# A gated recurrence in a three-layer kernel: states between chunks of 128 tokens in place of two levels of scores

## The reference

```python
# S_t = diag(f_t) S_(t-1) + k_t v_t^T,  o_t = S_t^T q_t,  k_t = 1 - f_t
G = jnp.cumsum(log_f, axis=3)            # within a chunk
q_dec, k_inv = q * jnp.exp(G), k * jnp.exp(-G)
k_to_end = k * jnp.exp(G_last - G)
o_intra = tril(q_dec @ k_inv.T) @ v
def step(state, xs):
    o_inter = jnp.einsum('bhtd,bhdv->bhtv', q_c, state)
    new_state = decay_c.T * state + jnp.einsum('bhsd,bhsv->bhdv', k_c, v_c)
    return new_state, o_inter
...
o = o * rsqrt(mean(o * o) + eps) * norm_g * sigmoid(o_gate)
```

## Time and profile before

| | us |
|---|---|
| median of three runs | 1473.52 |
| lowest, highest | 1471.86, 1474.23 |
| span of the profiled execution | 1473.2 |
| TensorE matmuls busy in it | 1439.7 |
| VectorE busy | 959.1 |
| ScalarE busy | 867.1 |
| GpSimd busy | 64.6 |

### The profile page before, as it was taken

How to read it: one execution, slowest core, us unless ns; L and a number is a source line. 1 busy time by engine, 2 the same in 40 slices (tenths; PEclk the granted TensorE clock), 3 DMA queues, 4 the chain that set the end, 5 groups by cost and what they waited for, 6 DMA issues and landing times.

```text
span 1473.2 us, 25050 instructions
## 1 busy us (share of the span) xinstructions
PE 1439.7 (98%) x10188; PEld 933.4 (63%) x10188; DVE 959.1 (65%) x1928; ACT 867.1 (59%) x1250; POOL 64.6 (4%) x150
## 2 busy tenths in 40 slices
PE   7999999999999999999999999989999999899998
PEld 4444477566468448576688764646785755466677
DVE  6732556888589666565677423678667246799974
ACT  6554456777654665454563553557665466778863
POOL 0000000000000100000010000001000000000000
PEclk9999999999999999999999999999999999999999
DMA  6323223113322423342323223321134332100002
GB/s 193 108 92 114 86 94 104 62 58 115 114 87 86 160 87 128 109 137 86 115 86 114 88 87 97 105 86 31 33 98 133 118 115 86 58 2 2 2 5 98
DMA packets 128531, 131.93 MB, mean 90 GB/s; under 512 B 9913, under 2 KB 125409, under 8 KB 128289
## 3 DMA queue, kind: packets, MB, share of 16 engines
q1 hardware_dynamic: 126096, 121.62, 25.9%
q0 software_dynamic: 2320, 8.71, 1.7%
HBM read 128.18 MB, written 2.10 MB: 88 GB/s over the span
## 4 chain that ended last, share of the span: by engine, by line
PE 79%; DVE 11%; ACT 5%; issue 3%; DMA 1%; SPq 0%; POOL 0%; DVEq 0%; ACTq 0%
PE bank L734 12%; PE bank L735 12%; PE bank L736 12%; PE bank L777 8%; PE bank L779 8%; PE bank L778 8%; PE bank L996 3%; PE bank L978 3%; PE bank L960 2%; DVE tmin L2520 1%; DVE wring L1971 1%; ACT whigh L1344 1%; PE bank L1059 1%; PE bank L1155 1%; PE bank L857 1%
## 5 line engine op out<-in xcount | busy, mean ns | idle before, releaser
L734 PE MATMUL bank<-xT,whigh 128*128 128x512 f16 x952 | 361.4, 380 | 1.1 <-DVE wring L1971 1.1
L735 PE MATMUL bank<-xT,whigh 128*128 128x512 f16 x952 | 361.3, 380 | 0.0
L736 PE MATMUL bank<-xT,wring 128*128 128x512 f16 x952 | 361.1, 379 | 0.0
L1971 DVE SCALAR_TENSOR_TENSOR wring<-wring,wsc,whigh 128x2048 f16<-128x2048 f32 (+2 forms) x106 | 245.2, 2313 | 137.5 <-ACT whigh L1344 137.0
L1344 ACT ACTIVATE whigh<-wring,wsc 128x2048 f16<-128x2048 f32 (+2 forms) x106 | 209.0, 1972 | 118.8 <-DVE wsc L1874 99.9
L1361 ACT ACTIVATE whigh<-wring 128x2048 bf16<-128x2048 f32 (+2 forms) x106 | 199.1, 1878 | 93.8 <-DMA wring<-in_w_down 27.9
L777 PE MATMUL bank<-whigh,slab 128*128 128x256 f16 x800 | 218.0, 273 | 2.3 <-DVE wring L1971 1.8
L779 PE MATMUL bank<-whigh,slab 128*128 128x256 f16 x800 | 218.1, 273 | 0.0
L778 PE MATMUL bank<-wring,slab 128*128 128x256 f16 x800 | 218.0, 273 | 0.0
L734 PEld LDWEIGHTS bank<-xT,whigh 128*128 128x128 f16 x952 | 93.3, 98 | 113.6 <-issue 3.3
L736 PEld LDWEIGHTS bank<-xT,wring 128*128 128x128 f16 x952 | 93.2, 98 | 112.7 <-issue 0.6
(11 more groups left out here) (335 smaller groups left out, 2295.2 us busy)
## 6 DMA issues: line engine op xcount, KB each, us to landing
wring<-in_w_in SPq DMA_DIRECT2D x27, 1024.0 KB, 5.1
wring<-in_w_up SPq DMA_DIRECT2D x16, 1024.0 KB, 5.3
wring<-in_w_down SPq DMA_DIRECT2D x16, 1024.0 KB, 5.3
wring<-in_even_w_in SPq DMA_DIRECT2D x14, 1024.0 KB, 5.3
wring<-in_odd_w_in SPq DMA_DIRECT2D x14, 1024.0 KB, 5.1
wring<-in_w_a SPq DMA_DIRECT2D x4, 1024.0 KB, 5.4
wring<-in_w_out SPq DMA_DIRECT2D x4, 1024.0 KB, 5.3
wring<-in_even_w_out SPq DMA_DIRECT2D x4, 1024.0 KB, 5.2
```

The lines of the kernel that those rows point to most:

```text
L734: pe.matmul(bank, wh[:, k, wcol:wcol + width], xh[:, k, :], start=k == 0, stop=False)
L735: pe.matmul(bank, wh[:, k, wcol:wcol + width], xl[:, k, :], start=False, stop=False)
L736: mm = pe.matmul(bank, wl[:, k, wcol:wcol + width], xh[:, k, :], start=False, stop=k == KC - 1)
L1971: dve.scalar_tensor_tensor(low_of(i)[:, :, 0:m], loaded(i)[:, :, 0:m], wsc[:, n:n + 1], high_of(i)[:, :, 0:m], ALU.mult, ALU.subtract).the ...
```

## The change

The two upper levels (segments of 128 and 256 tokens in queries and keys, score banks 3 and 4) are replaced. TensorE turns the keys of the first three blocks of 128 tokens (`K[3]`, decayed to the block's end) into bank 3. ScalarE copies them to `prob` where the upper scores stood. TensorE multiplies them by the values into bank 4 (`hgrn_sums`), between the two gate projections of the next turn. VectorE chains the three results with the decay of a block (`hgrn_states`, behind the levels of the next head), and writes three states where nothing else of `prob` is read. `hgrn_pv` multiplies the values by the diagonal blocks only and adds state times `Q[3]` for blocks 1 to 3. GpSimd's load of x waits for the values of head 6, since `Q[3]` is now read by them.

```diff
+        def turned_keys(h, c):
+            return prob[:, 4 * (h % 2), (c + 1) * P:(c + 2) * P]
+
+        def state(h, c):
+            return prob[:, 4 * (h % 2) + 3, (c - 1) * P:c * P]
+
+        def chunk_decay(h):
+            return (segdec, mulq)[h % 2][:, 3, 0:TT]
...
-                    pool.wait_ge(s_("hg_lvl"), 5 * (HEADS_H - 1))
+                    pool.wait_ge(s_("hg_pv"), HEADS_H - 1)
...
+            def score_bank(h, i):
+                r = 5 * h + i
+                if r >= 4:
+                    h0, i0 = divmod(r - 4, 5)
+                    if i0 < 2:
+                        pe.wait_ge(s_("hg_evd"), 2 * h0 + i0 + 1)
+                    elif i0 < 4:
+                        pe.wait_ge(s_("hg_eva"), 2 * h0 + i0 - 1)
+                    else:
+                        pe.wait_ge(s_("hg_st"), h0 + 1)
+                return SA[r % 4]
             def hgrn_scores(h):
                 b = h % 2
-                K = [kT[:, h, :]] + [side[:, 9 * b + 1 + i, :] for i in range(4)]
-                Q = [qT[:, h, :]] + [side[:, 9 * b + 5 + i, :] for i in range(4)]
-                for i in range(5):
-                    r = 5 * h + i
-                    if r >= 4:
-
-                        h0, i0 = divmod(r - 4, 5)
-                        if i0 < 2:
-                            pe.wait_ge(s_("hg_evd"), 2 * h0 + i0 + 1)
-                        else:
-                            pe.wait_ge(s_("hg_eva"), 3 * h0 + i0 - 1)
-                    bank = SA[r % 4]
-                    pe.wait_ge(s_("hg_lv"), 5 * h + min(i + 1, 4) + (i >= 3))
+                K = [kT[:, h, :]] + [side[:, 9 * b + 1 + i, :] for i in range(3)]
+                Q = [qT[:, h, :]] + [side[:, 9 * b + 5 + i, :] for i in range(3)]
+                for i in range(4):
+                    bank = score_bank(h, i)
+                    pe.wait_ge(s_("hg_lv"), 4 * h + i + 1)
                     if i < 3:
                         for j in range(TT):
                             mm = pe.matmul(bank[:, j * P:(j + 1) * P], K[i][:, j * P:(j + 1) * P],
                                            Q[i][:, j * P:(j + 1) * P], start=True, stop=True)
-                    elif i == 3:
-
-                        pe.matmul(bank[:, 0:P], K[3][:, 0:P], Q[3][:, P:2 * P], start=True, stop=True)
-                        pe.matmul(bank[:, P:3 * P], K[4][:, 0:P], Q[4][:, 2 * P:4 * P], start=True, stop=True)
-                        mm = pe.matmul(bank[:, 3 * P:4 * P], K[3][:, 2 * P:3 * P], Q[3][:, 3 * P:4 * P],
-                                       start=True, stop=True)
                     else:
-                        mm = pe.matmul(bank[:, 0:2 * P], K[4][:, P:2 * P], Q[4][:, 2 * P:4 * P], start=True, stop=True)
+                        for j in range(TT - 1):
+                            mm = pe.transpose(bank[:, j * P:(j + 1) * P], K[3][:, j * P:(j + 1) * P], ident[:, :])
                     mm.then_inc(s_("hg_lvl"), 1)
+            def hgrn_sums(h):
+                bank = score_bank(h, 4)
+                pe.wait_ge(s_("hg_eva"), 2 * h + 2)
+                for c in range(TT - 1):
+                    mm = pe.matmul(bank[:, c * P:(c + 1) * P], turned_keys(h, c), vtok[:, c, h * P:(h + 1) * P], start=True, stop=True)
+                mm.then_inc(s_("hg_lvl"), 1)
             def hgrn_pv(h):
                 pe.wait_ge(s_("hg_evd"), 2 * h + 2)
-                pe.wait_ge(s_("hg_eva"), 3 * h + 3)
+                pe.wait_ge(s_("hg_eva"), 2 * h + 1)
                 if h >= 1:
                     pe.wait_ge(s_("hg_o"), h)
                 for j in range(TT):
-                    mm = pe.matmul(SB[0][:, j * P:], vtok[:, j, h * P:(h + 1) * P],
-                                   prob[:, 4 * (h % 2) + j, j * P:], start=j == 0, stop=j == TT - 1)
+                    pe.matmul(SB[0][:, j * P:(j + 1) * P], vtok[:, j, h * P:(h + 1) * P],
+                              prob[:, 4 * (h % 2) + j, j * P:(j + 1) * P], start=j == 0, stop=False, skip_group_check=True)
+                pe.wait_ge(s_("hg_st"), h + 1)
+                for j in range(1, TT):
+                    mm = pe.matmul(SB[0][:, j * P:(j + 1) * P], state(h, j), side[:, 9 * (h % 2) + 7, j * P:(j + 1) * P],
+                                   start=False, stop=j == TT - 1, skip_group_check=True)
                 mm.then_inc(s_("hg_pv"), 1)
...
-                for key in (("ga", "og"), ("og", "ga"))[h % 2]:
+                for at, key in enumerate((("ga", "og"), ("og", "ga"))[h % 2]):
+                    if at == 1 and h >= 1:
+                        hgrn_sums(h - 1)
...
-                bank = SA[(r + 1) % 4]
-                act.activation(prob[:, p0, P:4 * P], bank[:, 0:3 * P], ACT.Copy)
-                act.activation(prob[:, p0 + 2, 3 * P:4 * P], bank[:, 3 * P:4 * P], ACT.Copy).then_inc(s_("hg_eva"), 1)
-                act.wait_ge(s_("hg_eva"), own(s_("hg_eva")))
-                act.wait_ge(s_("hg_lvl"), r + 3)
-                act.activation(prob[:, p0 + 1, 2 * P:4 * P], SA[(r + 2) % 4][:, 0:2 * P], ACT.Copy).then_inc(s_("hg_eva"), 1)
+                act.activation(prob[:, p0, P:4 * P], SA[(r + 1) % 4][:, 0:3 * P], ACT.Copy).then_inc(s_("hg_eva"), 1)
...
-                    if l < 3:
-                        dve.tensor_tensor(segdec[:, l + 1, 0:n // 2], seg[:, :, 0], seg[:, :, 1], ALU.mult)
+                    dve.tensor_tensor(chunk_decay(h) if l == 2 else segdec[:, 2, 0:n // 2], seg[:, :, 0], seg[:, :, 1], ALU.mult)
...
-                    dve.wait_ge(s_("hg_lvl"), 5 * (h - 1))
+                    dve.wait_ge(s_("hg_pv"), h - 1)
...
-                for l in range(1, 4):
+                for l in (1, 2):
                     n, w = 32 >> l, CH << l
                     dve.wait_ge(dve_chain, joined)
-                    if l < 3:
-                        joins(l + 1)
+                    if l == 1:
+                        joins(2)
                         joined = own(dve_chain)
-                    dve.wait_ge(s_("hg_lv"), 5 * h + 1 + l)
-                    if l < 3:
-                        dve.tensor_tensor(by(Q[l + 1], n), by(Q[l], n), wide(mulq[:, l, 0:n], n, w), ALU.mult)
-                        ins = dve.tensor_tensor(by(K[l + 1], n), by(K[l], n), wide(mulk[:, l, 0:n], n, w), ALU.mult)
-                    else:
-
-                        dve.tensor_tensor(by(Q[4], 4)[:, 2:4, :], by(Q[3], 4)[:, 2:4, :], wide(mulq[:, 3, 2:4], 2, w), ALU.mult)
-                        ins = dve.tensor_tensor(by(K[4], 4)[:, 0:2, :], by(K[3], 4)[:, 0:2, :], wide(mulk[:, 3, 0:2], 2, w), ALU.mult)
-                    ins.then_inc(s_("hg_lv"), 1)
+                    dve.wait_ge(s_("hg_lv"), 4 * h + 1 + l)
+                    dve.tensor_tensor(by(Q[l + 1], n), by(Q[l], n), wide(mulq[:, l, 0:n], n, w), ALU.mult)
+                    dve.tensor_tensor(by(K[l + 1], n), by(K[l], n), wide(mulk[:, l, 0:n], n, w), ALU.mult).then_inc(s_("hg_lv"), 1)
+            def hgrn_states(h):
+                dve.wait_ge(s_("hg_lvl"), 5 * h + 5)
+                sums = SA[(5 * h + 4) % 4]
+                dve.tensor_copy(state(h, 1), sums[:, 0:P]).then_inc(dve_chain, 1)
+                dve.wait_ge(dve_chain, own(dve_chain))
+                dve.scalar_tensor_tensor(state(h, 2), state(h, 1), chunk_decay(h)[:, 1:2], sums[:, P:2 * P], ALU.mult, ALU.add).then_inc(dve_chain, 1)
+                dve.wait_ge(dve_chain, own(dve_chain))
+                dve.scalar_tensor_tensor(state(h, 3), state(h, 2), chunk_decay(h)[:, 2:3], sums[:, 2 * P:3 * P], ALU.mult, ALU.add).then_inc(s_("hg_st"), 1)
...
+                if 1 <= h <= HEADS_H:
+                    hgrn_states(h - 1)
```

More of the change, by code:

```diff
@@ L1188, in _ @@
             pe.wait_ge(s_("hg_evd"), 16)
-            pe.wait_ge(s_("hg_eva"), 24)
+            pe.wait_ge(s_("hg_eva"), 16)
             pe.wait_ge(s_("gated"), 6)
@@ L2265, in hgrn_levels @@
                 segdec_there = own(dve_chain)
-                dve.wait_ge(s_("hg_lv"), 5 * h + 1)
+                dve.wait_ge(s_("hg_lv"), 4 * h + 1)
                 dve.sem_inc(s_("hg_k1"), 1)
                 if h >= 2:
-                    dve.wait_ge(s_("hg_lvl"), 5 * (h - 1))
+                    dve.wait_ge(s_("hg_pv"), h - 1)
                 dve.tensor_tensor(by(Q[1], 16), by(Q[0], 16), wide(first, 16, 2 * CH), ALU.mult)
```

## The result

The changed kernel takes 1510.69 us (median of 4 runs, 1508.21 to 1510.91) against 1473.88 us (4 runs, 1471.86 to 1474.98) on the same chip: ratio 1.0248, 95% interval 1.0235 to 1.0262, slower. The forecast was 1500, 1490 to 1511. The time lies 0.3 us inside the range, 10.7 us above the likeliest value, and within the 1505 to 1514 us of the case that had been given 0.14 (a fall of the clock in each turn), not within the 1496 to 1505 of the main case. The profiled execution took 1510.52 us with a span of 1508.5.

What follows compares the result with a forecast made beforehand. TensorE bounds the kernel before; after, a loop of TensorE and ScalarE bounds the recurrence. Span 1473.2 + 21 (stage) + 6 (clock) = 1500.2, median 0.3 above, 1500.5, said as 1500 us; range 1490 to 1511.

Steps and rivals of the forecast that it cites:

- the case that had been given 0.14: Recurrence: stalling loop with a clock fall in each turn, or a slower VectorE; 1505 to 1514 us, chance 0.14.
- the main case: Recurrence: a stalling loop with some falls of the clock; 1496 to 1505 us, chance 0.55.
- the loop: Sums wait for ScalarE's copy, ScalarE for tile B queued behind them; 20.7 or 19.5 us per turn, against 17.36.
- tile B: Last 24 of a head's 48 projection matmuls on TensorE, 5.18 us, queued behind the waiting sums.
- The last head: Values of head 7, delayed by GpSimd's loads of x, end 15.2 us after head 6's start, before 14.7: +0.5.
- I take five falls, and 1.2 us for each: Clock term: TensorE's clock falls behind some of seven new pauses; +6 us, bounds 0 and 12.
- the bound of 1.7: Clock term: most that one fall can cost, 1.7 us, all its slow time lying on tile B.
- The transposes: TensorE's work per head: three transposes of keys, 0.217 us each, like a matmul of 128 columns.
- the cover is 1 us: VectorE: states end 17.0 us after L1344's start; the second half of the value matmuls needs them at 18.0.
- TensorE stays the bound: Rival: keys copied by the end of tile A, 5.1 us saved, 1468.4 us; chance 0.07 for 1467 to 1470.
- The rival of a gain: Same rival as "TensorE stays the bound": faster, 1468.4 us, if the copy ends before tile A; chance 0.07.
- tile A: First 24 of a head's 48 projection matmuls on TensorE, just ahead of the sums.

Runs made afterwards that it cites:

- e1: Changed kernel with ScalarE's copies of head h-1 (turned keys among them) moved between the logarithms and the exponentials of turn h: 1490.77 us, ratio 1.0114.
- e2: Changed kernel with TensorE's sums of head h-1 moved behind the second gate projection, directly ahead of the values: 1488.45 us, ratio 1.0100.
- e3: Changed kernel with 13 idle float32 matmuls of 128 columns ahead of the sums in turns 1 to 7: 1496.86 us, ratio 1.0165.
- e5: e1 plus, on VectorE, output of head h-2 and states of head h-1 in the middle of the levels of head h: 1467.79 us, ratio 0.9960.
- e8: Changed kernel with GpSimd's second load of x issued one reduction later: 1510.29 us, ratio 1.0246.
- e7: Changed kernel with 6 idle matmuls, in place of e3's 13, ahead of the sums in turns 1 to 7: 1500.70 us, ratio 1.0181.
- e4: e1 plus, on VectorE, the states of head h-1 made ahead of all levels of head h: 1475.43 us, ratio 1.0013.
- e6: e5 plus GpSimd's second load of x issued one reduction later: 1466.34 us, ratio 0.9955.

## Why the prediction was right, and where its size was off

**The mechanism: right, and shown.** The pauses stand ahead of L930, released by ScalarE's copy, in turns 1 to 7, and the eighth sums have none. Taking the lateness of the copy away (e1) or of its reader (e2) removes exactly these pauses. The distance without the clock is 20.86 and 19.78 us (e3) for 20.7 and 19.5. Two terms of the loop hit to 0.1 us: 11.19 for 11.2 on ScalarE, 3.60 for 3.6 up to L1368.

That 21.4 us came out for 21.0 is partly luck. In e3 the first turn gave +4.2 (forecast 4.1) and the six loops 121.45 us (forecast 120.6): the sums start about 0.15 us behind the copy and not 0.1, they take 5.92 with tile B and not 5.83, and ScalarE's block is 11.27 in even turns. The last head gave +0.34 for 0.5, and from there to the mark it was 0.35 shorter than in the kernel before. These offset one another.

**The step that failed: the clock, "I take five falls, and 1.2 us for each".** There were seven, at 2.2 us each: 15.5 us for 6 (2.1 and 14.9 against the measured 5.92). That put the kernel into the case of 0.14; that 1490 to 1511 still holds it, by 0.3 us, is partly luck. The number was wrong because, of the four pauses in the earlier trace rows, I let the two without a fall count for pauses of 3 to 4 us; all seven pauses, of 3.01 us and more, had one. The size was wrong, and beyond the bound of 1.7 that I gave, because I took it from falls like those in the earlier trace rows, a little under four microseconds. Three of the seven were like that (clock down for about 3.4 us, from 303.3 to 306.7 for one). Behind the four longer pauses it stayed down for about 6.8 us. The text priced that ("each further half microsecond in seven turns is 3.5 us") only in a rival at 0.14. The rule of the Trainium skill that I weighed, TensorE: Matmul & The Clock Gate, section HAM oscillation, said that gaps in a regular loop drop the clock and each burst begins cold. In this kernel the clock fell in all seven turns, in six before the sums began and in turn 3 0.4 us into them, so by this case it should have had the greater chance. e3 shows the price directly: 14.8 us in the turns, 15.8 at the mark.

**From the span to the time: 0.3 us added where 1.8 to 2.1 belong.** In every execution whose time and span are both on record, the time is 1.76 to 2.13 us above the span (1510.52 against 1508.5). By that the span of 1473.2 belongs to an execution near 1475.0 (an estimate), 1.1 above the median, which is most of the reason why the median rises by 36.8 and the span by 35.3.

**The transposes: a misread row, and harmless.** I took eight records in the earlier trace rows for four transposes of 0.217 us. They are eight, of 0.109 each. In the new stage three take 0.32 us (L922 at 314.80, L951 at 315.12). A head holds about 16.45 us of TensorE work and not 16.7. While TensorE waits for ScalarE this moves the pause and not the time; it matters once the waits are gone, and makes e5's gain 0.9 us per head where I counted 0.64. The work that changed took 2.15 us for the values and 1.32 for the two upper levels of scores (298.48 to 299.80) before, and takes 0.89 + 0.67 (values), 0.33 (transposes) and 0.67 (sums) in e5.

**VectorE: "the cover is 1 us", right, and the next wait.** The states cost 1.05 us (taken 1.0) and are hidden in the kernel after; in e3, with the clock up, they end 0.85 and 1.2 us ahead of their reader L943. With the pause at the sums gone they are late by 1.2 to 2.4 us in turns 1 to 7 (e1). I didn't say that; the rival "TensorE stays the bound" named only one point that decides, the copy. It needed a second one: with the copy in time the kernel is still 1.1% slower.

**The last head: right.** It was forecast at 15.2 us and takes 414.12 + 0.67 - 399.79 = 15.0. The mechanism is that of the text, and e8 takes 1.7 us of it away (L943 starts 412.10 - 399.50 = 12.60 behind the values in e8, 14.33 in the kernel after).

**The rival of a gain: refuted for this order, reached in another.** It stood at 1468.4 for a copy that ends before tile A does. In the kernel after it doesn't; in e5, with the states early besides, it does, at 1467.79. That the two times agree is in part chance: the sum had 0.64 us per head over eight heads, e5 has 0.90 per head over seven and a slower last head.

## What to carry to other kernels

When work is taken off the engine that bounds a stage, ask of each new result what its reader's engine has queued behind the wait, and whether the maker waits for just that: a copy 4 us late cost not 4 us once but 3 us in every turn. Then ask it again of the next maker in the chain, because moving one late result forward only shows the next. And price a pause of TensorE with what comes behind it: here two fifths of the loss were slow matmuls behind the pauses, and idle matmuls in the pause won 13.8 us back.

## What the runs showed of the hardware that was not expected

- In the stage every stall of TensorE of 3.01 us and more was followed by a clock of 1.2 GHz (seven in the kernel after, seven in e8). It stayed down for about 3.4 us or for about 6.8. In the kernel after 3.01 to 3.10 us had the shorter fall, 3.75 to 4.31 the longer, which began inside the stall; the cost was 1.5 to 1.8 us and 2.3 to 3.0 us. But the length doesn't fix which: in e8 a stall of 4.31 us passed at 1.00, the clock fell 1.0 us behind it and only for 3.4 us, and in e7 a stall of 2.98 us had 6.8.
- Below 3 us the length alone didn't decide whether. Ten stalls of 2.00 to 2.44 us in e1, e2 and e7 all had a fall, as had 2.98; 1.93 and two of 2.83 had none. Outside the stage 2.16 and 2.41 had none and 1.99 and 2.88 had one, and the stall that ends near 16 us had a fall where it took 2.74 to 2.77 us (after, e2, e4) and none where it took 1.60 to 2.44 (the eight others). What else does is open. In the cases without a fall at 2.83 us six idle matmuls had gone just ahead of the pause, but so they had at 2.98 and 2.42.
- A fall needs no stall: in the kernel before the clock fell at 1239.6 us with no wait of TensorE ahead of it, behind 2.4 us of small float32 matmuls (L1098, 64 x 31, from 1236.90). The prediction counted the falls near 990 and 1280 only.
- Falls 600 to 900 us behind the stage came and went: two in the kernel after, e6 and e3, three in before, e2, e4, e5, e7 and e8, four in e1. That is 1 to 2 us either way, as much as some of the effects measured here. Whether the change in the stage moves them or they differ from one execution to the next isn't shown; the second is likely in part, since the same kernel's executions differ in their mean clock (0.994 to 0.998 for the kernel before) and since the stall near 16 us, which no change touches, differs as said above.
- A transpose of a float32 block of 128 x 128 takes 0.108 us on TensorE, half of a float32 matmul of 128 columns (0.217).
